# A projection stage with a stepwise first token form, an earlier weight load and later sums of squares

## What is computed

```python
shift, scale, gate = jnp.split((jax.nn.silu(c) @ w_ada + b_ada)[:, None, :], 3, axis=-1)
h = x * (1 + scale) + shift
proj = h @ w_in
...
qb = l2norm(qkv[:, :, 0]) * (HEAD_DIM_B ** -0.5)
kb = l2norm(qkv[:, :, 1])
```

## Time and profile before

| | before |
|---|---|
| median of 3 runs | 2743.51 us (2743.24 to 2747.04) |
| profiled execution, its own time | 2737.61 us |
| its span on the core | 2735.8 us |
| PE busy | 2438.8 us (89%) |
| DVE busy | 1628.2 us (60%) |
| ACT busy | 1101.4 us (40%) |
| POOL busy | 230.8 us (8%) |

### The profile page before, as it was taken

How to read it: one execution, slowest core, us unless ns; L and a number is a source line. 1 busy time by engine, 2 the same in 40 slices (tenths; PEclk the granted TensorE clock), 3 DMA queues, 4 the chain that set the end, 5 groups by cost and what they waited for, 6 DMA issues and landing times. The chain is left out here.

```text
span 2735.8 us, 44312 instructions
## 1 busy us (share of the span) xinstructions
PE 2438.8 (89%) x16766; PEld 2148.8 (79%) x16766; DVE 1628.2 (60%) x3740; ACT 1101.4 (40%) x2220; POOL 230.8 (8%) x421
## 2 busy tenths in 40 slices
PE   4999999999899999999996996388877669999996
PEld 2777788888899898999995883377776369999775
DVE  5767765553537666665443663487774566774554
ACT  4444444444215344444443562245442133322443
POOL 0000000001111111000000000111110001111000
PEclk7999999999999999999998997688886679999998
DMA  6223233325323322332326254756524455656442
GB/s 236 92 94 123 92 110 108 120 81 171 101 80 99 98 91 90 107 106 96 107 86 253 109 204 165 184 130 162 128 65 142 135 169 176 189 154 215 131 139 73
DMA packets 249772, 356.29 MB, mean 130 GB/s; under 512 B 54932, under 2 KB 187764, under 8 KB 244312
## 3 DMA queue, kind: packets, MB, share of 16 engines
q1 hardware_dynamic: 191256, 233.85, 28.3%
q0 software_dynamic: 31920, 106.63, 10.4%
q10 hardware_dynamic: 26384, 12.98, 1.8%
HBM read 241.27 MB, written 112.11 MB: 129 GB/s over the span
## 5 line engine op out<-in xcount | busy, mean ns | idle before, releaser
L292 PE MATMUL ps_f<-m_lo,w_hi 128*128 128x272 f32 (+1 forms) x2436 | 792.9, 325 | 23.2 <-DVE m_lo L595 13.2
L292 PE MATMUL ps_f<-m_hi,w_hi 128*128 128x272 f32 (+1 forms) x2436 | 796.2, 327 | 0.0
L292 PE MATMUL ps_f<-m_hi,w_lo 128*128 128x272 f32 (+1 forms) x2436 | 787.7, 323 | 0.0
L292 PEld LDWEIGHTS ps_f<-m_lo,w_hi 128*128 128x128 f32 x2436 | 461.5, 189 | 78.6 <-issue 35.9
L292 PEld LDWEIGHTS ps_f<-m_hi,w_lo 128*128 128x128 f32 x2436 | 462.2, 190 | 37.3
L292 PEld LDWEIGHTS ps_f<-m_hi,w_hi 128*128 128x128 f32 x2436 | 461.1, 189 | 34.0
L659 DVE TENSOR_TENSOR stage<-partial,ps_f 128x512 f32<-128x512 f32 (+2 forms) x348 | 171.4, 506 | 328.6 <-PE ps_f L292 316.7
L417 ACT ACTIVATE partial<-ps_f 128x272 f32<-128x272 f32 (+1 forms) x348 | 161.5, 464 | 415.3 <-PE ps_f L292 414.0
L379 ACT ACTIVATE w_hi<-w_raw 128x512 fp32r<-128x512 f32 x348 | 213.7, 626 | 196.6 <-PE ps_f L292 127.1
L566 DVE TENSOR_TENSOR w_lo<-w_raw,w_hi 128x512 fp32r<-128x512 f32 x348 | 239.2, 688 | 87.7 <-ACT w_hi L379 84.1
L65 PE MATMUL ps_fm<-u_lo,w_tail_hi 128*128 128x256 f32 (+1 forms) x768 | 221.5, 288 | 11.7 <-DVE u_lo L2716 7.0
(11 more groups left out here) (384 smaller groups left out, 3965.4 us busy)
## 6 DMA issues: line engine op xcount, KB each, us to landing
w_raw<-in_w_feat SPq DMA_DIRECT2D x58, 1024.0 KB, 6.3
gates<-scratch_g_d SPq DMA_DIRECT2D x56, 256.0 KB, 3.2
z_f<-scratch_z_d ACTq DMA_DIRECT2D x16, 768.0 KB, 5.2
scratch_conv_d<-conv POOLq DMA_DIRECT2D x18, 544.0 KB, 3.0
scratch_conv_d<-conv POOLq DMA_DIRECT2D x18, 512.0 KB, 2.9
kc<-in_k_cache SPq DMA_DIRECT2D x8, 1152.0 KB, 14.3
vc<-in_v_cache SPq DMA_DIRECT2D x8, 1152.0 KB, 15.0
scratch_g_d<-stage POOLq DMA_DIRECT2D x16, 544.0 KB, 4.4
```

The costliest lines, as they stand in the source:

```text
L292: last = pe.matmul(out[:, 0:n], l[:, cols], r, start=start and k == 0 and nth == 0, stop=k == KH - 1 and nth == 2, skip_group_check=not start)
```

## The change

Four edits, all in `modulate_and_project`:

1. Quarter 11 of pass 0 is modulated by DVE (before: ACT), slice by slice; ACT rounds each slice when it is there, DVE takes the remainder of each, and product 0 of q = 0 waits for its slices one at a time. Each slice has its own signal.
2. The order of the forms' preparation in pass 0: s3 is combined before the remainder of 12 and before s1; ACT rounds s3, 22, s1, s2, then does `copy_out(0, 0, 0)` (f1_put), then rounds s4. Before, s3 was combined and rounded last and `copy_out(0, 0, 0)` came after all roundings. The remainder of s3 stays last.
3. `load_values(3)` is issued right after `load_values(2)`, ahead of `wait_value(sp, half_one)`.
4. `norms(q, 1)` runs after product 0 of pair q + 2 (before: after product 6 of pair q + 1), and `take_sums(q, 1)` follows accordingly, for both passes.

```diff
--- before.py
+++ after.py
@@ -170,6 +170,7 @@
         buf = lambda q, j: 2 * (q % 2) + j
         tile = lambda q, j: 2 * place(q) + j
         conv_no = lambda q, j: T_CONV * of_pass(q) + tile(q, j)
+        normed = lambda q: q >= 0 and has_norm(q)
         norm_no = lambda q, j: 2 * NHB * of_pass(q) + tile(q, j)
         steps_of = lambda s: (1 + s) * (TAPS - 1)
         steps_to = lambda q, j: T_CONV * steps_of(0) * of_pass(q) + steps_of(of_pass(q)) * (tile(q, j) + 1)
@@ -254,10 +255,10 @@
             for j in range(2):
                 sp.wait_ge(conv_stored[j], 16 * N_CONV)
             load_x(1, "11", xs[:, 0]), load_x(1, "12", xs[:, 2]), load_x(1, "21", xs[:, 1])
-            load_values(2)
+            load_values(2), load_values(3)
             wait_value(sp, half_one)
             load_x(1, "22", m_sum[slot(1, "22")][:, :, :])
-            for e in range(NG, 2 * NG):
+            for e in range(NG + 1, 2 * NG):
                 load_values(e)
             for q in range(NPAIR, NQ):
                 load_raw(q)
@@ -283,9 +284,11 @@
                 m, x = forms(s)[j]
                 if u == 0:
                     pe.wait_ge(w_lo_done[j], q + 1)
-                if first:
+                if first and (s, m) != (0, "11"):
                     pe.wait_ge(m_lo_done[s, m], 1)
                 for k in range(KH):
+                    if first and (s, m) == (0, "11"):
+                        pe.wait_ge(m_lo_done[s, m], k + 1)
                     cols = slice(P * k, P * (k + 1))
                     hi, lo = m_hi[x][:, k, at:at + n], m_lo[x][:, k, at:at + n]
                     for nth, (l, r) in enumerate(((wh[j], lo), (wl[j], hi), (wh[j], hi))):
@@ -312,6 +315,8 @@
                     pe.wait_ge(c21, n)
                     pe.wait_ge(c22, n)
                 product(q, u, 0, a, first, True)
+                if u == 0 and normed(q - 2):
+                    norms(q - 2, 1)
                 if n:
                     pe.wait_ge(c11, n)
                 product(q, u, 1, b, first, True)
@@ -323,14 +328,12 @@
                 if U:
                     pe.wait_ge(f4_put, U)
                 product(q, u, 4, D_BANK, first, True)
-                if last and q and has_norm(q - 1):
+                if last and normed(q - 1):
                     norms(q - 1, 0)
                 pe.wait_ge(f3_put, U + 1)
                 product(q, u, 5, c, first, False)
                 pe.wait_ge(f2_put, U + 1)
                 product(q, u, 6, a, first, False)
-                if last and q and has_norm(q - 1):
-                    norms(q - 1, 1)
 
             def value(v):
                 s, g, b = VB[v]
@@ -474,18 +477,25 @@
             act.wait_ge(ada_done, 1)
             act.activation(rows, N_BANK[:, :], ACT.Copy).then_inc(row_put, 1)
             a11, a12, a21 = xs[:, 1], xs[:, 2], xs[:, 0]
-            modulated(0, "11", a11), rounded(0, "11", a11, [(x_mod[0, "11"], 1)])
+            for k in range(KH):
+                act.wait_ge(x_mod[0, "11"], k + 1)
+                act.activation(m_hi[0][:, k, 0:HT], a11[:, k, 0:HT], ACT.Copy).then_inc(m_hi_done[0, "11"], 1)
             modulated(0, "12", a12), rounded(0, "12", a12, [(x_mod[0, "12"], 1)])
             low = lambda s, m: m_sum[slot(s, m)][:, :, :]
             modulated(0, "22", low(0, "22"))
-            for m in ("s1", "s2", "22", "s4", "s3"):
-                rounded(0, m, low(0, m), [(x_mod[0, m], 1)] if m == "22" else [(sum_put[0, m], 1)])
+            rounded(0, "s3", low(0, "s3"), [(sum_put[0, "s3"], 1)])
+            rounded(0, "22", low(0, "22"), [(x_mod[0, "22"], 1)])
+            for m in ("s1", "s2"):
+                rounded(0, m, low(0, m), [(sum_put[0, m], 1)])
+            copy_out(0, 0, 0)
+            rounded(0, "s4", low(0, "s4"), [(sum_put[0, "s4"], 1)])
             for q in range(NPAIR):
                 nxt = q + 1 < NPAIR
                 if q:
                     split(q, 6)
                 after(q - 1, 0), after(q - 1, 1)
-                copy_out(q, 0, 0)
+                if q:
+                    copy_out(q, 0, 0)
                 if nxt:
                     split(q + 1, 0)
                 after(q - 1, 2)
@@ -739,20 +749,24 @@
             put(dve.tensor_scalar(mods[:, KT:, :], mods[:, KT:, :], 1.0, None, ALU.add), mod_ready)
             dve.wait_ge(mod_ready, 2)
             a11, a12, a21, a22 = xs[:, 1], xs[:, 2], xs[:, 0], low(0, "22")
-            remainder(0, "11", a11)
-            remainder(0, "12", a12)
+            dve.wait_ge(x_in[0, "11"], 16)
+            for k in range(KH):
+                put(dve.tensor_scalar(a11[:, k, 0:HT], a11[:, k, 0:HT], mods[:, KT + k, 0:1], mods[:, k, 0:1], ALU.mult, ALU.add), x_mod[0, "11"])
+            for k in range(KH):
+                dve.wait_ge(m_hi_done[0, "11"], k + 1)
+                put(dve.tensor_tensor(m_lo[0][:, k, 0:HT], a11[:, k, 0:HT], f32(m_hi[0][:, k, 0:HT]), ALU.subtract), m_lo_done[0, "11"])
             dve.wait_ge(x_in[0, "21"], 16)
             for k in range(KH):
                 last = dve.tensor_scalar(a21[:, k, 0:HT], a21[:, k, 0:HT], mods[:, KT + k, 0:1], mods[:, k, 0:1], ALU.mult, ALU.add)
             put(last, x_mod[0, "21"])
             s1, s2, s3, s4 = (low(0, m) for m in ("s1", "s2", "s3", "s4"))
+            combine(0, "s3", s3, a11, a21, ALU.subtract, [(x_mod[0, "21"], 1), (x_mod[0, "11"], KH)])
+            remainder(0, "12", a12)
             combine(0, "s1", s1, a21, a22, ALU.add, [(x_mod[0, "21"], 1), (x_mod[0, "22"], 1)])
-            combine(0, "s2", s2, s1, a11, ALU.subtract, [(sum_put[0, "s1"], 1), (x_mod[0, "11"], 1)])
+            combine(0, "s2", s2, s1, a11, ALU.subtract, [(sum_put[0, "s1"], 1), (x_mod[0, "11"], KH)])
             remainder(0, "s1", s1)
             combine(0, "s4", s4, a12, s2, ALU.subtract, [(sum_put[0, "s2"], 1), (x_mod[0, "12"], 1)])
-            remainder(0, "s2", s2), remainder(0, "22", a22), remainder(0, "s4", s4)
-            combine(0, "s3", s3, a11, a21, ALU.subtract, [(x_mod[0, "21"], 1)])
-            remainder(0, "s3", s3)
+            remainder(0, "s2", s2), remainder(0, "22", a22), remainder(0, "s4", s4), remainder(0, "s3", s3)
             for b in range(4):
                 dve.memset(stage[:, b, 0:S_PRE], 0.0)
             for q in range(NPAIR):
@@ -761,6 +775,7 @@
                     add(q - 1, 0, 1, 0), add(q - 1, 0, 1, 1)
                     rest(q, 6)
                 convolve(q - 1, 0)
+                take_sums(q - 2, 1)
                 add(q, 0, 0, 0)
                 if nxt:
                     rest(q + 1, 0), weigh(q + 1, "T1"), rest(q + 1, 1), weigh(q + 1, "T3")
@@ -771,7 +786,6 @@
                 add(q, 0, 0, 1)
                 if nxt:
                     rest(q + 1, 5)
-                take_sums(q - 1, 1)
             add(NPAIR - 1, 0, 1, 0), add(NPAIR - 1, 0, 1, 1)
             rest_of_values(0)
             a11, a12, a21, a22 = xs[:, 0], xs[:, 2], xs[:, 1], low(1, "22")
@@ -823,6 +837,8 @@
                     add(prev, 1, 1, 0), add(prev, 1, 1, 1)
                     rest(q, 6)
                 convolve(prev, 0)
+                if prev > NPAIR:
+                    take_sums(prev - 1, 1)
                 add(q, 0, 0, 0)
                 add(q, 0, 0, 1)
                 add(q, 0, 1, 0), add(q, 0, 1, 1)
@@ -835,7 +851,6 @@
                 add(q, 1, 0, 1)
                 if nxt:
                     rest(q + 1, 5)
-                take_sums(prev, 1)
             add(NQ - 1, 1, 1, 0), add(NQ - 1, 1, 1, 1)
 
         @block.gpsimd
```

## The result

| | before | after |
|---|---|---|
| median, us (lowest to highest of 4 runs) | 2743.74 (2743.24 to 2747.04) | 2702.86 (2701.03 to 2705.76) |
| profiled execution, us (its span) | 2737.6 (2735.8) | 2703.76 (2702.0) |
| busy PE / DVE / ACT in the span, us | 2438.8 / 1628.2 / 1101.4 | 2431.6 / 1630.7 / 1094.5 |
| last matmul of the projection stage starts, us | 1445.4 | 1408.4 |
| from there to the end of the span, us | 1290.4 | 1293.6 |

The ratio is 0.985, with an interval of 0.983 to 0.987: the kernel is 40.9 us faster. The forecast of 2704.5 us lies 1.6 us above the measured median.

A forecast was written before the change was run, and what follows sets the result against it. PE, the engine that waits at the edited places, was taken to bound the kernel; 12.0 + 13.4 + 13.7 = 39.1 us, so 2743.5 - 39 = 2704.5 us, range 2696.5 to 2712.5.

The forecast's parts named there:

- The first pair: Start of pass 0, edits 1 and 2: second pair begins at 67 instead of 78.95 us; gain 12.0 us, bounds 10.0 to 13.4.
- the 4.7 us at the first product: PE's first product starts at about 33.6 instead of 38.3 us; not the gain, since PE will stand again.
- the price of cutting up: DVE's first chain: four pieces cost about 0.2 us more than one; by the skill page some 0.5 to 0.9 us.
- The values: Value part, edit 3: the 10.8 us bank wait and 2.7 us of slow clock go; gain 13.4 us, bounds 12.7 to 13.5.
- The bound on quarter 22: Pass 1, behind the value loads: quarter 22 is modulated 0.7 us after DVE wants it, hidden by two free banks.
- The sums: Pass 1, edit 4: six waits shortened, 8.8 us, and clock drops gone, 4.9 us; gain 13.7 us, bounds 8.8 to 17.6.
- The slow stretches: Pass 1: after three of the six waits the clock is 0.52 for 3.4 us, costing 1.6 us each; expected to go.
- one sign of being wrong: The prediction is wrong if the stages after the projection are not as long as before.
- later stages answer to the shift: Rival: clock drops after the projection fall differently, 3 us to either side; chance 0.06 for this alone, more than 3 us off.

The follow-up runs named there:

- f2_first: The changed kernel with ACT's copy of product 3 ahead of the weight rounding, in the first pair only; 2701.17 us, ratio to the kernel before 0.9839.
- step_only: The kernel before with edit 1 alone: form 11 in four pieces, old order of the other forms; 2739.27 us, ratio 0.999.
- order_only: The kernel before with edit 2 alone: the new order, form 11 modulated and split whole; 2732.95 us, ratio 0.9964.
- norms_only: The kernel before with edit 4 alone: second sums after product 0 of the pair after next; 2725.02 us, ratio 0.993.
- start_only: The kernel before with edits 1 and 2 alone, without the fourth value load and the moved sums; 2727.76 us, ratio 0.9936.
- value_only: The kernel before with edit 3 alone, the earlier load of the value weights; 2728.32 us, ratio 0.9941.

## Why the prediction was right

**The first pair (12.0, measured 12.8 and, alone, 12.3).** The working holds step by step. The forecast was made with the vectors of before, so 1.4 us are taken off here. The last remainder then ends at 59.9, forecast 60.6; product 3 starts at 53.4, forecast 54.5; PE waits 1.07 us for ACT's copy, forecast 1.4, and f2_first shows that it is this copy. Most of the 0.8 us by which the pair was better lie in one step: DVE was to stand until 35.9 for quarter 21, and it goes on at 35.0 (36.44 in the profile, right behind the four remainders) without a wait. Of product 2 only a part runs at the low clock, which the prediction had for the whole: its matmuls last 0.39 us from 50.74 on and 0.63 us from 51.93 on (up to the row at 54.06). The way in which the 12.8 us come about is more than DVE's chain: its last remainder ends 6.9 us earlier behind the vectors than before (29.3 us against 36.2), and the rest is that products 3 to 5 now run while DVE still works, where before product 3 stood until 65.02 for ACT's copy. PE's first matmul comes 2.9 us behind the vectors, forecast 3.0. What the split into step_only and order_only adds is the share: 2.5 us for the steps, 10.5 us for the order. The prediction had said that the 4.7 us at the first product are not the gain, and the measured 2.5 us agree, within the 1.3 us by which this stretch varies.

On the price of cutting up: the four remainders take 2.49 us from the first start to the last end (34.03), a whole one 2.29 us, so cutting costs 0.2 us. By the Trainium skill (VectorE: DVE Perf Modes, the TRN2 errata), whose fixed part of each instruction would be paid three times more, it would be 0.47 us, an estimate from its (N + 151) / 0.96 ns. The durations agree with that formula (0.69 and 2.29 us); but the starts of neighbours lie only some 0.60 us apart. Here the measurement decides.

**The values (13.4, measured 13.4).** v = 17 to v = 21 is 11.20 us instead of 24.61, in the whole change and alone. The bound on quarter 22 (0.7 us) was drawn from the right mechanism, but neither its size nor the two banks that were to hide it held in every profile: DVE waits 0.21 and 1.15 us, PE none and 0.74 us.

**The sums (13.7, measured 13.3; alone 13.7).** The six waits are 4.1 us, forecast 3.9, and the slow stretches are gone. The slow stretches were put at 1.6 us each and cost 1.5 us. The 0.4 us by which the whole change falls short of norms_only are the waits themselves, 4.1 us against 3.7: the third is 0.97 us long, where the others are 0.62 to 0.66. Why that one is longer, no run here shows.

**What the prediction did not have.** Two pieces. After the 3.7 us wait at the start of the values the clock stayed at 0.53 for 6.8 us instead of 3.4 us: 1.1 us lost in the changed kernel, in both of its profiles, and also in start_only, value_only and step_only, but not in norms_only, order_only or f2_first; as f2_first has all four edits and 3.4 us, it is tied to none of them. And the modulation vectors came 1.4 us later; over the profiles here they come between 30.58 and 33.51 us, with kernels that touch nothing ahead of them, so this belongs to the single execution.

**The median was met with some luck.** In the profiled executions the difference is 33.9 us, not 39.1. The three terms came to 39.5 us (12.8, 13.4 and 13.3), and from that go 1.4 us for the later vectors, 1.1 for the clock at the values and 3.2 for the rest of the kernel. In the medians it is 40.9 us. The two differ because the profiled execution of before, 2737.6 us, lies below every other run of it taken here (2739.72 to 2749.79), while that of the changed kernel lies among its own. Which part of the kernel before is longer in those other runs, no profile here shows; this stays open.

The parts tell the same. By their own marks in the profiles they add up: 12.3 + 13.4 + 13.7 = 39.4 us against 39.5 for the whole. By the ends of the stage, behind the vectors, they give 10.0 + 10.9 + 15.3 = 36.2 us against 38.4, since each profile also holds what its part does not touch: longer waits and slow stretches later on (start_only, value_only), the first pair 1.3 us shorter (norms_only). By the medians they give 16.7 + 16.1 + 19.4 = 52.2 us against 41, and here the cause is open. So the three terms are shown by their marks in the profiles; the sum in the median is shown only to the 5 us or so by which the base is uncertain.

**The rest of the kernel.** It was 1290.4 us before and is 1293.6 us after. By the letter one sign of being wrong came true, that the stages after the projection are not as long as before. Over all thirteen profiles the rest lasts 1289.6 to 1294.8 us (on average 1291.3) in the eight whose stage ends after 1427 us, and 1291.9 to 1297.2 (on average 1294.5) in the five whose stage ends before 1410 us. So the rival "later stages answer to the shift" is not excluded: some 3 us may have been given back there, which is the size that the prediction gave it. The two groups overlap, so it is not shown either. The sum had 0 for it.

## What to carry to other kernels

When a start-up chain binds, follow the engine with the longest chain and put its work in the order in which the consumer needs it, the copies that free a bank included; that an earlier first matmul wins little shows only if the whole chain is counted. A wait of some 2 us ahead of thin matmuls should be priced with the slow clock that can follow it: removing the standing won both here, while removing the thin matmuls was not tried. And measure from marks inside the profile as well as by the median: a single profiled execution may lie 6 us from its kernel's own median, which is as much as half of a term.
